# Attention slots regrouped: transposes, dense steps together, products with V, then scores; 15 slots in place of 16

## The reference

```python
def fox_attention(q, k, v, log_f):
...
    s = jnp.einsum('bqhd,bkhd->bhqk', qi, k).astype(jnp.float32) * scale
    s = s + ci[..., None] - c[:, :, None, :]
    p = masked_softmax(s, kpos[None, :] <= t[:, None])
    return jnp.einsum('bhqk,bkhd->bqhd', p.astype(v.dtype), v)

def nsa_attention(q, k_c, v_c, k_s, v_s, k_w, v_w, gates, pe, w1, w2):
...
    s_c = jnp.einsum('bqgrd,bngd->bgrqn', qi, kc).astype(jnp.float32) * scale
    p_c = masked_softmax(s_c - slopes[None, :, :, None, None] * d_c, d_c >= 0)
    o_c = jnp.einsum('bgrqn,bngd->bqgrd', p_c.astype(dt), vc)
...
```

## Time and profile before

| | us |
|---|---|
| median of the runs (lowest, highest) | 1760.7 (1757.25, 1761.7) |
| span of the profiled execution | 1757.1 |
| PE busy | 1679.6 (96%) |
| DVE busy | 916.1 (52%) |
| ACT busy | 627.2 (36%) |
| the four attention passes, 700.3 to 913.8 of the span | 213.5 |

### The profile page before, as it was taken

The page is one execution under the profiler, slowest core; times in us unless marked ns, Lnnn a source line. Parts: engine busy times, 40 slices in busy tenths (PEclk is TensorE's granted clock), DMA queues, the critical chain, the costliest instruction groups (busy, mean ns, idle before and its releaser), DMA issues.

```text
span 1757.1 us, 22185 instructions
## 1 busy us (share of the span) xinstructions
PE 1679.6 (96%) x8263; PEld 1311.8 (75%) x8263; DVE 916.1 (52%) x1376; ACT 627.2 (36%) x946; POOL 225.3 (13%) x204
## 2 busy tenths in 40 slices
PE   1999899999999999999999999999998999999996
PEld 1757688888888867666667788888887688888885
DVE  6765676544334463666667544444336644444223
ACT  1324334222223362554555333333226333333221
POOL 5010106998000030000000000003000000000000
PEclk9999999999999999999998999999999899999998
DMA  7565134454332241111101322233211133333221
GB/s 281 204 200 167 40 110 161 169 181 157 109 107 97 69 117 64 37 37 49 37 25 61 108 96 95 95 100 115 98 57 49 61 98 100 99 96 115 92 80 48
DMA packets 48588, 179.27 MB, mean 102 GB/s; under 512 B 5968, under 2 KB 6640, under 8 KB 48272
## 3 DMA queue, kind: packets, MB, share of 16 engines
q1 hardware_dynamic: 43600, 162.04, 27.5%
q0 software_dynamic: 3776, 14.78, 2.7%
q10 hardware_dynamic: 1152, 1.66, 0.4%
HBM read 173.04 MB, written 2.10 MB: 100 GB/s over the span
## 4 chain that ended last, share of the span: by engine, by line
PE 71%; issue 22%; DVE 5%; DMA 1%; ACT 1%; ACTq 1%; POOL 0%; POOLq 0%; DVEq 0%; SPq 0%
PE bank L383 15%; PE bank L385 14%; PE bank L384 14%; PE bank L1437 3%; PE bank L1439 2%; PE bank L1438 2%; PE bank L1545 2%; PE bank L1501 2%; PE bank L1521 2%; DVE ada_acc L1972 1%; PE bank L1172 1%; PE bank L1174 1%; PE bank L1173 1%; PE bank L454 1%; PE bank L1394 1%
## 5 line engine op out<-in xcount | busy, mean ns | idle before, releaser
L309 DVE TENSOR_TENSOR w_lo<-raw,w_hi 128x1024 fp32r<-128x1024 f32 (+1 forms) x229 | 316.4, 1382 | 575.2 <-ACT w_hi L305 574.9
L305 ACT ACTIVATE w_hi<-raw 128x1024 fp32r<-128x1024 f32 (+1 forms) x229 | 258.0, 1127 | 564.4 <-PE bank L385 482.7
L383 PE MATMUL bank<-h_hi,w_hi 128*128 128x512 f32 x1136 | 448.0, 394 | 0.5 <-DVE w_lo L309 0.5
L385 PE MATMUL bank<-h_hi,w_lo 128*128 128x512 f32 x1136 | 442.2, 389 | 0.0
L384 PE MATMUL bank<-h_lo,w_hi 128*128 128x512 f32 x1136 | 442.2, 389 | 0.0
L383 PEld LDWEIGHTS bank<-h_hi,w_hi 128*128 128x128 f32 x1136 | 213.2, 188 | 50.2 <-issue 5.2
L385 PEld LDWEIGHTS bank<-h_hi,w_lo 128*128 128x128 f32 x1136 | 213.2, 188 | 45.0
L384 PEld LDWEIGHTS bank<-h_lo,w_hi 128*128 128x128 f32 x1136 | 213.3, 188 | 44.6 <-issue 1.7
L383 PE MATMUL bank<-hid_hi,w_hi 128*128 128x512 f32 x528 | 205.6, 389 | 0.0
L384 PE MATMUL bank<-hid_lo,w_hi 128*128 128x512 f32 x528 | 205.4, 389 | 0.0
L385 PE MATMUL bank<-hid_hi,w_lo 128*128 128x512 f32 x528 | 205.4, 389 | 0.0
(11 more groups left out here) (397 smaller groups left out, 2079.5 us busy)
## 6 DMA issues: line engine op xcount, KB each, us to landing
raw<-in_f2i SPq DMA_DIRECT2D x88, 512.0 KB, 3.3
raw<-in_ffi SPq DMA_DIRECT2D x44, 512.0 KB, 3.4
raw<-in_f2o SPq DMA_DIRECT2D x32, 704.0 KB, 4.0
ada_w<-in_ada_w SPq DMA_DIRECT2D x24, 512.0 KB, 4.3
m_out<-in_ada_w POOLq DMA_DIRECT2D x24, 512.0 KB, 3.7
raw<-in_att_w SPq DMA_DIRECT2D x23, 512.0 KB, 3.3
raw<-in_ffo SPq DMA_DIRECT2D x16, 704.0 KB, 4.0
raw<-in_ada_w SPq DMA_DIRECT2D x16, 512.0 KB, 4.9
```

What stands on the lines that cost most here:

```text
L305: nc.scalar.activation(WH[par][:, 0:kc * P], RAW[s][:, 0:kc * P], ACT.Copy).then_inc(whi, count)
L309: nc.vector.tensor_tensor(WL[par][:, 0:kc * P], RAW[s][:, 0:kc * P], WH[par][:, 0:kc * P].bitcast(F32), ALU.subtract).then_inc(wlo, count)
L383: pe_.matmul(bank[:, :], w_h, hi[:, k0 + k, :], start=start and k == 0, stop=False)
L385: last = pe_.matmul(bank[:, :], w_l, hi[:, k0 + k, :], start=False, stop=stop and k == kc - 1)
```

## The change

Passes 1 to 4 get 15 slots. `GROUPS` allows several pairs in one slot of work, but here each group holds one pair, in the order of before, so that `NG_` is 13 and every `off` is 0. The instructions are the same ones with the same sizes (the same number on every engine); what changes is their order.

- PE's slot is `turn(sl - 2)`, all its dense steps, the early output step, `pv(sl - 2)`, `qk(sl)`. `pv` moves from three slots behind `qk` to two.
- ACT's slot is `take(sl - 2)`, then `exp(sl - 1)` (was `exp(sl)`).
- DVE's slot is `score(sl - 1)` (was `score(sl)`), the low part of a weight block, `norm(sl - 1)`, and the finished dense block behind it.
- Passes 1 to 3 have 3, 3 and then 2 dense steps in every slot. In the last pass the twelve early output steps are one in each of slots 3 to 10, one in slot 14 and three behind the last slot.

```diff
-        SLOTS = 16
-        STEPS = [[2] * 12 + [0] * 4] + [[3, 3, 2, 2, 2, 2, 1, 2, 2, 2, 1, 2, 2, 2, 2, 2]] * 3 + [[3, 3, 2] + [0] * 13]
-        EARLY_AT = 3
...
+        SLOTS = [16] + [NG_ + 2] * 4
+        STEPS = [[2] * 12 + [0] * 4] + [[3, 3] + [2] * 13] * 3 + [[3, 3, 2] + [0] * 12]
+        EARLY_STEPS = [0, 0, 0] + [1] * 8 + [0, 0, 0, 0]
...
+            for p in range(1, 5):
                 it = p - 1
-                for sl in range(SLOTS):
-                    steps = chunk_of[p, sl]
-                    ahead = (len(steps) + 1) // 2
-                    for s_ in steps[:ahead]:
+                for sl in range(SLOTS[p]):
+                    if sl == 1:
+                        fv_turn(it)
+                    if sl >= 2:
+                        turn(it, sl - 2)
+                    for s_ in chunk_of[p, sl]:
                         lin_step("att6", s_ // C, s_ % C)
...
-                        if sl < NP_:
-                            qk(it, sl)
-                    for s_ in steps[ahead:]:
-                        lin_step("att6", s_ // C, s_ % C)
-                    if p > 0:
-                        if 2 <= sl < NP_ + 2:
-                            turn(it, sl - 2)
-                        if 3 <= sl < NP_ + 3:
-                            pv(it, sl - 3)
+                    if p == 4:
+                        if sl == 3:
+                            pe_.wait_ge(a6["ol"], 6)
+                        early_steps(EARLY_STEPS[sl] if sl < SLOTS[p] - 1 else 1)
+                    if sl >= 2:
+                        pv(it, sl - 2)
+                    if sl < NG_:
+                        qk(it, sl)
+            early_steps(len(early))
...
-                        if 2 <= sl < NP_ + 2:
+                        if sl >= 2:
                             take(it, sl - 2)
-                        if sl < NP_:
-                            exp(it, sl)
-                        if sl == 7:
+                        if 1 <= sl <= NG_:
+                            exp(it, sl - 1)
+                        if sl == FOX_GROUP + 3:
                             out_hi(it, 0)
...
+                for sl in range(SLOTS[p]):
+                    if p and 1 <= sl <= NG_:
+                        score(it, sl - 1)
+                    if p and sl == 0 and it:
+                        out_lo(it - 1, 1)
+                    for j in ready_at.get((p, sl - 1) if sl else (p - 1, SLOTS[p - 1] - 1), ()):
+                        att_split(j)
+                    if p and 1 <= sl <= NG_:
+                        norm(it, sl - 1)
```

More of the change, by code:

```diff
@@ L862, in build_program, with part_of @@
                     if _s % C == C - 1:
[L863 to L869, removed]
+                        ready_at.setdefault((_p, _sl), []).append(_s // C)
+        FOX_GROUP, CMP_GROUP = 3, 4
+        def part_of(tile, slot, half, off, n):
+            return tile[:, slot, S * half + off:S * half + off + n]
         blk = ctx.enter_context(nc.Block())
@@ L1495, in qk @@
                             q = slice(64 * half, 64 * half + 64)
-                            pe_.matmul(QB[:, half, 0:L], SELB[q, 2 * it + half, :], CR[q, 0:L], start=True, stop=False)
+                            pe_.matmul(QB[:, half, off:off + L], SELB[q, 2 * it + half, :], CR[q, 0:L], start=True, stop=False)
                     for half in range(2):
@@ L1524, in pv @@
[L1524 to L1547, removed]
@@ new lines, in _, with early_steps @@
+            EARLY = [k for k in range(C) if k % 4 < 3]
+            early = [(j, k, e == 0) for j in range(2) for e, k in enumerate(EARLY)]
+            def early_steps(count):
+                for j, k, first in early[:count]:
+                    lin_step("att_out", j, k, first, False)
+                del early[:count]
+            for sl in range(SLOTS[0]):
+                steps = chunk_of[0, sl]
+                ahead = (len(steps) + 1) // 2
+                for s_ in steps[:ahead]:
+                    lin_step("att6", s_ // C, s_ % C)
+                cmp_tail(sl)
+                for s_ in steps[ahead:]:
+                    lin_step("att6", s_ // C, s_ % C)
@@ L1857, in exp, with take @@
[L1857 to L1873 removed]
+            def take(it, g):
+                G_ = NG_ * it + g
+                act.wait_ge(a6["tr"], pairs_before(G_ + 1))
+                if G_ >= 2:
+                    act.wait_ge(a6["pv"], pairs_before(G_ - 1))
+                x, kind, i, off = MEMBERS[g][-1]
+                rows, L = (NCMP, S) if kind == "cmp" else (P, off + (i + 1) * P)
+                dst = PT[0:rows, G_ % 2, :].rearrange("p (h s) -> p h s", h=2)
+                act.activation(dst[:, :, 0:L], TB[0:rows, :, 0:L], ACT.Copy).then_inc(a6["pt"], len(MEMBERS[g]))
@@ new lines, in exp @@
+            def exp(it, g):
+                G_ = NG_ * it + g
+                for x, kind, i, off in MEMBERS[g]:
+                    X_ = NP_ * it + x
+                    if kind == "cmp":
+                        act.wait_ge(a6["sc"], 2 * X_ + 2)
+                        sc = SC[:, G_ % 4, 0:2 * TC * NCMP]
+                        act.wait_ge(a6["cs"], 3 * it + 3)
+                        act.activation(sc, sc, ACT.Exp).then_inc(a6["ex"], 2)
+                    else:
+                        for half in range(2):
+                            act.wait_ge(a6["sc"], 2 * X_ + 1 + half)
+                            sc = part_of(SC, G_ % 4, half, off, (i + 1) * P)
+                            col = 2 * x + half
+                            act.activation(sc, sc, ACT.Exp, scale=-1.0, bias=AST[:, 0, col:col + 1],
+                                           accum_out=AST[:, 1, col:col + 1]).then_inc(a6["ex"], 1)
```

247 lines of the change are left out of this document (120 added, 127 removed).

## The result

The changed kernel takes 1783.8 us (median of 4 runs, 1783.4 to 1785.4) against 1759.5 us for the kernel before, measured with it (the median that the prediction started from, 1760.7, was of three runs). The ratio is 1.0141, with a 95% interval of 1.0127 to 1.0155: 24 us slower. The forecast was 1780 with a range of 1771 to 1789. The profiled execution has a span of 1781.7 us, 24.6 more than before.

The account below looks back on a forecast made before the run. PE, busy 96% of the span, was taken as the bound, with a one-slot loop making it wait: 14.6 - 8.4 - 0.6 + 10.0 + 0.6 = +16.2, +3 for handovers, so 1760.7 + 19, rounded to 1780 us; range 1771 to 1789.

Parts of the forecast that it names:

- a ring of one slot: Transposes, copy, next pair's exponentials, scaling and transposes form a loop closing every slot; PE's other work only covers it.
- PE's handovers: In full passes, grouping two dense steps saves an entry and an exit per slot, 2.3 us of PE's work.
- The ring's links: Lengths of the loop's steps on PE, ACT and DVE; hardest turn 4.79 us, twelve turns of a full pass 46.9.
- 0.1 for each of seven chain steps: Allowance for unpriced handovers where the chain decides; over 32 such steps +3 us, with ends 0 and +6.
- The gap between passes: Last transposes of a pass to the first of the next: 10.2 us instead of 13.01, -8.4 for three.
- 4.9 - 2.8 + 0.7 = 2.8: Net loss of a full pass: 4.9 us on its turns, less the shorter gap, plus the handover allowance.
- the table load: Pass 1: ACT's 1.28 us load moves onto the chain before the first exponentials; with 1.9 saved ahead, -0.6 together.
- "+10.0": Last pass: PE's cover is gone, so its twelve turns take 45.4 us instead of 35.4.
- "+0.6": Behind the last pass's turns: four early output steps instead of one precede the wait for the last results.
- The clock rival: Granted clock falls in the last pass, whose PE work takes up to twice as long: +30 us, 1810; chance 3%.
- The other rivals: PE waits nowhere, 1752, 4%; only the last pass loses, 1764, 4%; weight splits fall into the loop, 1787 likelier, 6%.
- The signs: Right: full passes 57 to 59 us, transposes waiting 4 to 7, last about 13. Wrong: 53 us passes, split waits, clock under 1.00.

Follow-up runs that it names:

- experiment 4: Against the changed kernel: passes 1 to 3 with transposes, copy and products one slot later than scaling allows for two slots, last pass as before; 1753.5 us, ratio 0.9957.
- experiment 6: Changed kernel with a dummy two-column exponential ahead of the copy of V in slot 0 of pass 1; 1781.2 us.
- experiment 9: Kernel before with the change in the last pass only; 1774.5 us, ratio 1.0083.
- experiment 3: Changed kernel with one early output step in each of slots 3 to 14 of the last pass; 1782.1 us, ratio 1.0118.

## Why the prediction was right

The mechanism, the sign and the time were right: a ring of one slot closes over all three engines, PE waits for it, and the time fell in the range, at 24 us instead of 19. That the range held it is in part luck: it was made up from the size of the steps and the spread of the runs, and the 5 us that were missing came from the clock, for which it had no term. Step by step:

- **PE's handovers save 2.3 us a full pass.** Measured: PE's busy time in a full pass is 52.8 instead of 55.1, and with the ring open a pass is 2.1 us shorter (experiment 4). The Trainium skill, "TensorE: Matmul & The Clock Gate", section "Step-by-step: what each phase is for", says that weight loads are pulled ahead of matmuls in flight. Whatever that hides, the way into and out of a group of dense matmuls is not hidden here: it takes 0.32 and 0.34 us, against the 0.23 from one dense matmul to the next.
- **The ring's links.** The hardest turn, 512 keys behind the compressed pair, was priced at 4.79 and took 4.82. From the first to the last transposes of pass 2 (768.79 to 816.32 on PE's timeline) it is 47.5 us; the working gave 46.9 and 0.1 for each of seven chain steps, 47.6.
- **The gap between passes** was to be 10.2 and is 10.12 (816.32 to 826.44). A full pass so costs 2.6 us more than before, against 4.9 - 2.8 + 0.7 = 2.8 forecast.
- **Pass 1** was to pay 1.3 us on top for the table load. It paid 2.9 (experiment 6): 1.4 ahead of its first transposes, so the load was right, and 1.5 behind them, where the clock behind the long wait was missing.
- **The last pass is the step that was mis-sized.** "+10.0" for its twelve turns, 11.1 with the handovers, was 14.6 (884.09 to 934.06, 50.0 us, against 35.4 before), and "+0.6" behind it 1.3. The ring's turns were right where the clock was 1.00: 899.62 to 904.43 is 4.81 for the hardest again. The missing 3.5 us lie where it fell: the turns of 128 behind 512 keys, forecast at 4.0 each, took 5.17 and 5.70 at the low clock, and 4.08 at 1.00 (914.12 to 918.20 in experiment 9); the last turn took 4.40 instead of 3.66.
- **The clock rival** had 3%, as a fall over the whole of the last pass with +30 us. It came in part, in three stretches. Summed over pass 1 (1.5) and the last pass (about 4) it is the 5 us between the 19 forecast and the 24 measured. The Trainium skill, "TensorE: Matmul & The Clock Gate", section "A second HAM failure mode: psum-queue depth-cycling", tells of short idles between matmul groups that make the gate swing. The trace agrees, at 0.54 of full clock for 921 to 935, but not for waits as such: passes 2 and 3 wait for 4.8 us each at a clock of 1.00. The fault was to give the clock one case, all or nothing, where a partial fall belonged into the sum.
- The other rivals fell: PE did wait, in the full passes too, and it never waited for a split.
- **The signs.** Of those named for "right", the full passes, their waits and PE's busy time came as said. In the last pass the transposes waited for only 7.4 us of the 13 named, and the products for another 3.3. One sign named for "wrong" came as well: a granted clock under 1.00, in the first and the last pass.

What stays open is what lets the clock fall. Experiment 9 prices the last stretch, 2.4 us, but its clock too was low for the final 3 us of it, so the whole price may be more. Why the clock fell at 922 in the changed kernel and held for some six microseconds longer over the same instructions and waits in experiment 9 no run shows. A filler without any use between the products was not tried.

## What to carry to other kernels

When work is reordered over several engines, write down for each engine which instruction stands behind which, and look for rings: the time around a ring, divided by the number of slots that it spans, is the shortest slot, whatever the engines' shares of busy time. Here the pipeline's depth was worth more than a tidier slot, and the tidier slot paid once the depth was kept (0.4%). And where waits are to appear on PE, put a partial fall of the clock into the sum; here it was about a fifth of the loss.

## What the runs showed of the hardware that was not expected

The granted clock fell after a single wait of 2.15 us (pass 1 of the changed kernel) and stayed at 1.00 through two passes with eight waits of 0.4 to 0.9 us each. With one dense step in each slot it held at 1.00 over 921 to 940 although PE was busy for only 13.3 of 19 us (experiment 3), while without them it was 0.54 although PE was busy for 10.7 of 14. It would be easy to take the missing dense steps for the cause, but experiment 9 has the same slots without them, in the same order and behind the same waits, and its clock was 1.00 for their first 8 us (914 to 922, PE busy for 5.1). So the same sequence of instructions and waits was met by a fall in one profile and not in another. And the code ahead of attention, the same in all these kernels up to one dense step, does not always take the same time: the first scores began between 702 and 707 us in these profiles. No run was made to find out why.
